# One word in the order of the scalar engine: where the exponential of the attention sink stands among the heads of a windowed attention

## The reference, cut to what matters

```
s_sink = jnp.broadcast_to(sink..., s_band.shape[:-1] + (1,))
p = jax.nn.softmax(jnp.concatenate([s_band, s_ctx, s_sink], -1), axis=-1)
p_band = p[..., :3 * BLK]
p_ctx = p[..., 3 * BLK:3 * BLK + C]
o = einsum(p_band, vb) + einsum(p_ctx, vc)
```

## Time and profile before

| | us |
|---|---|
| median of 3 runs | 2426.77 (2426.15 to 2429.72) |
| the profiled execution's own time | 2426.15 |
| its span in the profile | 2424.1 |

### The profile page before, as it was taken

How to read it: one execution, slowest core, us unless ns; L and a number is a source line. 1 busy time by engine, 2 the same in 40 slices (tenths; PEclk the granted TensorE clock), 3 DMA queues, 4 the chain that set the end, 5 groups by cost and what they waited for, 6 DMA issues and landing times. The chain is left out here.

```text
span 2424.1 us, 42135 instructions
## 1 busy us (share of the span) xinstructions
PE 1857.7 (77%) x12030; PEld 1083.7 (45%) x12031; DVE 1569.1 (65%) x1965; ACT 976.5 (40%) x1253; POOL 359.4 (15%) x346
## 2 busy tenths in 40 slices
PE   6879999962426999699991099999999999999300
PEld 1157677641115777455551044544444444454100
DVE  1264444447897999676767343657669998655387
ACT  2023232136455888422220223445537776533110
POOL 0000000000001222121221500211111211111154
PEclk8989999986667999898895599999999999999755
DMA  9521111011104111233321743668869999848475
GB/s 362 200 57 45 61 39 48 19 40 37 37 35 182 61 62 47 82 118 130 111 105 20 175 172 126 235 238 305 312 240 396 400 398 398 317 160 325 156 243 207
DMA packets 169583, 406.06 MB, mean 168 GB/s; under 512 B 19349, under 2 KB 32053, under 8 KB 168501
## 3 DMA queue, kind: packets, MB, share of 16 engines
q1 hardware_dynamic: 146904, 326.69, 37.7%
q0 software_dynamic: 13120, 44.06, 5.4%
q10 hardware_dynamic: 9504, 34.61, 3.6%
HBM read 329.73 MB, written 75.60 MB: 167 GB/s over the span
## 5 line engine op out<-in xcount | busy, mean ns | idle before, releaser
L1814 PE MATMUL ps<-arena 128*128 x1200 | 457.2, 381 | 33.5 <-DVE arena L1734 32.8
L1734 DVE SCALAR_TENSOR_TENSOR arena<-arena 128x2048 f32 (+1 forms) x186 | 419.3, 2288 | 89.2 <-ACT arena L1667 48.4
L1815 PE MATMUL ps<-arena 128*128 x1200 | 457.0, 381 | 0.0
L1816 PE MATMUL ps<-arena 128*128 x1200 | 456.9, 381 | 0.0
L558 PE MATMUL ps<-arena 128*128 128x256 f16 (+1 forms) x2448 | 326.0, 296 | 21.5 <-DVE arena L469 21.5
L1661 ACT ACTIVATE arena<-arena 128x2048 f32 (+1 forms) x124 | 232.5, 1907 | 164.3 <-PEq L1413 66.0
L558 PEld LDWEIGHTS ps<-arena 128*128 128x128 f16 x2448 | 242.1, 100 | 99.8 <-issue 17.3
L1814 PEld LDWEIGHTS ps<-arena 128*128 128x128 f16 x1200 | 117.9, 98 | 174.3 <-issue 47.5
L1816 PEld LDWEIGHTS ps<-arena 128*128 128x128 f16 x1200 | 117.9, 98 | 139.2 <-issue 2.2
L1815 PEld LDWEIGHTS ps<-arena 128*128 128x128 f16 x1200 | 117.8, 98 | 130.7 <-issue 2.3
L823 PE MATMUL ps<-arena 128*128 128x512 f32 (+1 forms) x160 | 76.6, 644 | 109.2 <-DVE arena L728 72.2
(11 more groups left out here) (247 smaller groups left out, 2899.3 us busy)
## 6 DMA issues: line engine op xcount, KB each, us to landing
arena<-w SPq DMA_DIRECT2D x186, 1024.0 KB
y_d<-arena ACTq DMA_DIRECT2D x50, 512.0 KB, 6.2
arena<-w_mod SPq DMA_DIRECT2D x12, 2048.0 KB, 8.3
arena<-x SPq DMA_DIRECT2D x8, 1024.0 KB, 5.3
arena<-x SPq DMA_DIRECT2D x16, 512.0 KB, 4.6
x_d<-arena SPq DMA_DIRECT2D x16, 512.0 KB, 2.6
h_d<-arena SPq DMA_DIRECT2D x16, 512.0 KB, 3.0
arena<-x_d SPq DMA_DIRECT2D x16, 512.0 KB, 5.5
```

The source lines that it names most:

```text
L1734: return nc.vector.scalar_tensor_tensor(dst, src, scale, high, ALU.mult, ALU.subtract)
L1814: pe.matmul(out, high, part(buf, whi, at, 512), start=first, stop=False)
L1815: pe.matmul(out, high, part(buf, wlo, at, 512), start=False, stop=False)
L1816: return pe.matmul(out, low, part(buf, whi, at, 512), start=False, stop=last)
```

## The change

One number in the order of ACT changes: `exp_sink` goes from 0 to -2. The sink's exponential of a tile is now emitted two head steps later, behind `high_p` of head 0' instead of behind `high_p` of head 6.

```
-            pairs(act, ((exponent, 0), (high_p, -1), (exp_sink, 0)))
+            pairs(act, ((exponent, 0), (high_p, -1), (exp_sink, -2)))
```

## The result

| | before | after |
|---|---|---|
| median, us | 2426.46 (2426.13 to 2429.72, 4 runs) | 2469.74 (2468.05 to 2472.49, 4 runs) |
| the profiled execution's own time | 2426.15 | 2464.56 |
| its span | 2424.1 | 2462.7 |
| ratio | | 1.0176, 95% interval 1.0158 to 1.0194 |

The change makes the kernel 43.3 us slower; 41.9 had been forecast (23.9 for the wait and 18.0 for the clock). The profiled execution is 3.5 us faster than the fastest of the four in the median, and 38.4 us slower than the profiled one before; what is read from its rows adds up to that.

A forecast was written before the change was run, and what follows sets the result against it. Bound taken: a chain at each attention tile end, where whatever holds normalise back holds the whole pipeline. 2426.15 + 23.9 (wait) + 18.0 (PE's clock) = 2468.1 us, 2468.7 for the median; own range 2456 to 2480, widened to 2449 to 2480.

The forecast's parts named there:

- the wait: At 15 attention tile ends normalise waits for POOL's power, 1.53 us each, 23.0; with 0.97 at the phase's end, 23.9.
- the clock: PE falls to half clock behind the attention's stalls: 12 spells of 1.5 us, 18.0 us, between 0 and 28.6.
- the term's own bound of 24.2: Upper bound for the delay at 15 tile ends, without the 0.03 and with 1.61 us everywhere; lower bound 20.9.
- the handover from POOL to DVE: Time from the power's end on POOL to the start of the waiting DVE instruction, taken as 0.10 us.
- the phase's end: End of the attention: the sink's exponential now stands behind the last high_p, making normalise 0.97 us later.
- The estimate of 0.88 for `values` at half clock: On PE, values was estimated to take 0.88 us at half clock, against 0.44 at full clock.
- The choice of 12 from 11 falls in 14 stalls: Output phase's ratio of half-clock falls to stalls, applied to the attention's 15 stalls, giving 12 spells.
- The clock holds (1): In the steady attention, the same wait but no half-clock spells: 2450.7 us, chance 0.18.
- The gap soaks up the delay (2): ACT's idle time at each tile end absorbs the delay, leaving 0.2 us a tile: 2431 us, chance 0.05.
- Nothing changes (3): POOL has room and no engine gets added work, so the kernel stays at 2427 us; chance 0.03.
- Faster (4): Taking the exponential out of ACT's tight steps gives back up to 0.10 us in 16 tiles: 2425.2 us, chance 0.03.
- slack of 1.77 us: In the kernel before, normalise on DVE starts 1.77 us after POOL's power (L952) ends.

The follow-up runs named there:

- (4): Changed kernel with POOL's power (L952) replaced by a product with a small constant, leaving out the division: 2422.43 us, ratio 0.9987.
- (5): Kernel before, sink's exponential at its early place, POOL taking the power three times in a row instead of once: 2475.64 us, ratio 1.0217.
- (1): Kernel before with exp_sink at -1 instead of 0, one head step later instead of two: 2430.06 us, ratio 1.0021.
- (7): Changed kernel with low_p ahead of normalise on DVE instead of behind it: 2442.39 us, ratio 1.0077.
- experiment 3: Changed kernel with PE doing the scores of head 5 of each tile four times instead of once: 2452.13 us, ratio 1.0112.
- experiment 2: exp_sink at -3, three head steps later than in the kernel before, one more than in the changed kernel: 2511.32 us, ratio 1.0355.

## Why the prediction was right, point by point

**The wait.** Right in its place and cause. The releaser of `normalise` changed as said (profile after), the loss vanishes with a short last step on POOL while the sink stays late (4), appears with the sink early (5), is nearly nothing while the slack lasts (1), and each time L1058 is released by POOL. The prediction let the delay pass through `low_p`; that is the way in the changed kernel (`transposes` wait 2.77 us for it), but with `low_p` ahead the wait for the emptied bank passes on nearly as much (7). The size was too small: 1.53 us a tile were forecast. The tiles without a spell are 16.13 us apart and 16.10 in experiment 3, against 14.43 before ((968.14 - 766.14) / 14, from the first to the fifteenth `normalise`), so 1.70 and 1.67, and 15 times that is above the term's own bound of 24.2. The term of the sum that was mis-sized is the handover from POOL to DVE. It was taken as 0.10 from the earlier trace rows and measured 0.20 to 0.23 at the 12 tile ends inside the loop, in the changed kernel and in experiments 2 to 5 and 7. With 0.21 the working gives 1.64; what made the other 0.03 to 0.06 was not tried. At the first and the last three tile ends, which are written out outside the loop, the handover is only 0.03 to 0.04, as here, one kernel's timeline of POOL and DVE (after the change):

```profile
986.99 1.64 POOL L952 TENSOR_TENSOR small<-small 128x8 f32<-128x8 f32 x1 [0.28 <-POOL small L947]
...
988.66 0.69 DVE L1058 SCALAR_TENSOR_TENSOR arena<-ps,small 128x512 f32<-128x512 f32 x1 [2.13 <-POOL small L952]
```

At the phase's end DVE idles 1.66 us before the last `normalise`, against 0.77: 0.89 where 0.97 was forecast, and 0.90 with a handover of 0.03. Together some 26 instead of 23.9.

**The clock.** Right in kind, and near in size. 12 spells of 1.5 us were forecast, 18.0. In the profile there are 11, and a tile with one takes 17.50 us on average against 16.13, so 1.37 each and 15.1 together. Experiment 3 takes them all away and gains 16 to 18 in the timed runs; how many spells these have is not recorded. The estimate of 0.88 for `values` at half clock was measured as 0.82. The choice of 12 from 11 falls in 14 stalls of another phase came out near, but it is a count by analogy, and that phase has a twelfth fall, behind the part that was counted. Why 4 stalls have no spell was not tried. The prediction was right not to lean on the advice of the Trainium skill (TensorE: Matmul & The Clock Gate, Why this matters for your kernels), by which a gap of this size would still pass: here 11 of 15 gaps of 2.6 to 2.8 us had half clock beside them, and this measurement decides.

**The total.** That it was met to 1.0 us is in part luck. For an execution like the profiled one 2468.1 was forecast, and it took 2464.56. There the wait was 2 us more than reckoned and the clock 3 less, the attention began 1.4 earlier (below), and the phases behind it took 1.2 less.

**Rivals.** The clock holds (1): refuted by 0.93 and by experiment 3, which shows what that rival would have been, 2452.1 where it said 2450.7. The gap soaks up the delay (2): refuted, ACT's break grew from 1.27 or 1.42 to 2.98 us at the full clock, by the whole delay. Nothing changes (3): refuted; POOL was busy 45 of 235 us and still sets the pace once a tile. The advice of the Trainium skill (Perfetto Trace Analysis, Identifying the Most-Contended Engine), to find the bottleneck by occupancy, would have passed POOL over. The next step of the Trainium skill (Perfetto Trace Analysis, Optimization Strategy), to look for the gaps of the busy engine and for what blocks it there, finds the place: DVE waits 2.0 us for L952. Faster (4): refuted. That the power had a slack of 1.77 us was right to within 0.1: with 1.65 used up by the move and 0.20 by the handover, a tile grew by 0.08 (1).

**Signs.** 16.0 and 17.5 us between the starts of L1058 were forecast, 16.1 and 17.5 measured; 2.0 us of idle time on DVE, 2.00 to 2.21 measured; 0.1 from L952 to `normalise`, 0.03 outside the loop and 0.20 to 0.23 inside it measured. ACT's break was forecast at 2.9 and 3.5 us: 2.98 and 3.97. The second was too small: `transposes` and `values` of head 0' both run at half clock inside the break and are 0.52 and 0.38 us longer, 0.90 together, where 0.6 was reckoned. The two terms add to 41, and the attention ends 39.8 later: it also began its steady rhythm 1.4 us earlier in this execution (the first `high_p` is at 749.60, before at 750.99). PE had the full clock there from 747.4 on; in the kernel before it was at half clock until about 753.

## What to carry to other kernels

A small step on an idle engine can be moved for nothing up to its slack and at full price, once for each turn of the loop, beyond it; the slack is the time from the end of the last small step to the start of the instruction that waits for it, less the handover. Ask of every wait what is queued behind it: the order of two instructions on DVE is worth 7 us in the kernel before and 24 to 27 in the changed one, about half of that through the clock. Then ask what else waits for the late instruction, since the delay can pass that way too. Where a wait opens a gap on PE, reckon with the clock as a second term, and part the two by giving PE harmless work in the gap.

## What the runs showed that I had not expected

The handover from POOL's power to the waiting DVE instruction was 0.20 to 0.23 us at the 12 tile ends inside the loop, 0.03 outside it, and 0.10 in the earlier trace rows. The register instruction L1055, with the wait for the power, runs 12 times in the changed kernel, from 783.6 to 970.9, just at these tile ends, and L1057 with another wait stands between it and `normalise`. That fits, but no run changed it. Of 15 PE gaps of 2.6 to 2.8 us, 11 had half clock for 3.4 us beside them; of the 15 of 2.7 to 3.0 us in experiment 5, 12 had; gaps of 1.0 to 1.35 us in front of `transposes` (experiments 1, 3 and 4 and the kernel before) never had; the gaps of 4.3 to 4.8 us of experiment 2 always, for 6.5 to 7.0 us in 14 of 15 cases. And a gain in one phase can be partly lost in the next without any change there: 11.3 us earlier out of the attention, 4.2 us more in the output phase.
